# A two-layer, two-block network on one core: expert rows through a DRAM table and four indirect gathers, and a reordered start

## The chip, the cores and the metric

One NeuronCore of a Trainium2 chip runs one program, one launch. The metric is the device time of that program in microseconds (us), lower is better. TensorE (PE), VectorE (DVE), ScalarE (ACT), GpSimd (POOL) and SyncE (SP) run their own instruction streams and wait for each other by semaphores; transfers are issued by SP, ACT and POOL.

## The reference, cut to what matters

A first block (two layers of attention beside a long convolution) and a second block (two layers) are applied to 256 tokens of width 1024. All is float32. The change touches the very start of the first block (its RMS norm and its position bias) and the last stage of the second one, a mixture of experts:

```python
def moe_swiglu(h, w_router, w_gate, w_up, w_down):
    logits = (h @ w_router).astype(jnp.float32)
    top_val, top_idx = lax.top_k(logits, TOP_K)          # 2 of 8 experts for each token
    weights = jax.nn.softmax(top_val, axis=-1)
    gates = jnp.sum(jax.nn.one_hot(top_idx, N_EXPERTS, dtype=jnp.float32) * weights[..., None], axis=-2)
    out = jnp.zeros_like(h)
    for e in range(N_EXPERTS):
        out = out + gates[..., e:e + 1] * swiglu(h, w_gate[e], w_up[e], w_down[e])   # 1024 -> 2816 -> 1024
    return out
...
        y = moe_swiglu(h, o_router[j], o_exp_gate[j], o_exp_up[j], o_exp_down[j])
        x = x + (g * y).astype(x.dtype)
    return rmsnorm(x, final_norm).astype(x.dtype)
```

In the first block, `h = rms_norm(x, pre_norm[l])` opens each layer, `rel_bias[bucket]` gives the position bias of the attention, and the filters of the long convolution are `sin` layers times `exp(-t * |deltas|)` (the decay rates).

## The kernel before, in words

Every engine's stream is written by hand in one order; nothing reorders it. The program goes through the first block's two layers (a list of steps, `STEPS`), the even layer of the second block with a feed-forward of 11 chunks, the state-space layer, the router, and then the experts. All transfers of weights are issued by SP, in one order, each behind a wait for the slot of its ring to be free; small ones are issued by ACT.

**The expert loop.** The router's result is cut on the device into work items: an item is one expert and up to 96 of its tokens (`SLOTS`). With these inputs there are 8 items. The loop (`nc.Fori`, over a count read from `itab`) runs one item a turn on PE, ACT, DVE and SP. On PE an item is:

- `lone()`, one small job, and then 8 waves (`wave(w)`, 32 matmuls of 512 columns each in four column groups; a float32 matmul has two records in the trace, so 64 records): the up and gate products of the item's tokens with the expert's weights. The weights come in 11 chunks `wgu` of 2 MB in four slots.
- `lone_sum()` behind wave 0: it needs `xpart`, which ACT copies out of PSUM (`xp_ready`).
- **`back(i)`** behind wave 0: four 128x512 matmuls that add the rows of the *previous* item back to their tokens. Their left side is `ptb`, the one-hot matrix of who sits in which slot, turned by `turn_slots`; their result is scaled by the gate and added to `x` by DVE in `taken_back`. For item 0 the rows are zeros. One more `back` stands behind the loop.
- `turn(w)`, transposes of a wave's result; **`turn_slots(i)`** behind wave 1, four transposes of the one-hot matrix.
- `down(c)` for 11 chunks `wdn` of 1 MB, behind the waves.
- **`gather(i + 1)`** behind wave 7: 16 small matmuls that pick the next item's tokens; in the last item they pick nothing that is used.

SP issues a chunk when PE has let go of its slot: chunk 4 (`load_up(i, e, 4)`) waits for the end of wave 0, and wave 2 waits for that chunk. In the chunk numbers that wait first, wave 5 needs chunks 7 and 8 and wave 6 chunk 9.

DVE ends an item by writing `ysb`, the item's 96 rows scaled by the layer's gate (two operations of 128x512; the PSUM tile holds the 96 rows in six pieces of 32 partitions).

**The start.** SP issues x (1 MB), constants, weights chunk 0, more constants, weights chunks 1 to 3. ACT issues `rel_bias`, a table, `vec` (the norm gains and other vectors), `flt_deltas` (the decay rates, 1 MB) and `flt_w_out`; then copies and stores the bias row, then waits for x **and `vec`**, and squares x for the norm. Behind the norm it issues eight reads of the stored row (`skewed`), which PE needs at the step `bias` behind its third group of projections.

## Time and profile before

| | before |
|---|---|
| median of 3 runs | 2069.11 us (2068.7 to 2070.05) |
| the profiled execution, its own time | 2067.41 us |
| its span | 2065.6 us |
| mean granted TensorE clock | 0.985 of full speed |
| PE / DVE / ACT / POOL busy | 97% / 32% / 18% / 5% of the span |
| DMA, mean over the span | 229 GB/s |

Busy shares are means over stages with different limits. PE is the engine with nearly no idle time, so what matters for each part of a change is whether it stands in PE's stream, or makes PE wait.

### The profile page before, as it was taken

What the parts mean: (1) busy time and instruction counts of PE and PEld (TensorE: products, weight loads), DVE (VectorE), ACT (ScalarE), POOL (GpSimd) and SP (SyncE); (2) the same over time, 40 slices, a digit from 0 to 9 for tenths busy, and PEclk for the clock granted to TensorE, in tenths of its full rate; (3) what the DMA queues carried; (4) which work ended last, traced back from release to release, by engine and by line L of the source; (5) the groups of instructions that cost most, each with busy time, mean ns of one, the idle gap of its engine ahead of it and who ended that gap; (6) DMA issues with size and microseconds to landing.
All of it is one profiled execution on the core that took longest, in us unless ns stands there. A gap on an engine that the chain in (4) does not pass through costs nothing.

```text
span 2065.6 us, 28841 instructions
## 1 busy us (share of the span) xinstructions
PE 1998.3 (97%) x12128; PEld 1104.6 (53%) x12128; DVE 659.8 (32%) x1436; ACT 379.0 (18%) x784; POOL 111.1 (5%) x94
## 2 busy tenths in 40 slices
PE   6999999999998999999989988999999999999998
PEld 5577775667774865777756544232323333333332
DVE  3265113345212474344449934010101010111112
ACT  3212103212102232243320012010101010111101
POOL 0000000000000000000016610000000000000000
PEclk9999999999999999999999998999999999999999
DMA  8245575344665223243323125989898979797973
GB/s 316 82 163 204 217 282 202 116 156 171 234 265 228 82 82 150 115 175 131 123 102 123 41 102 217 376 329 374 324 384 330 381 309 403 311 402 298 406 299 148
DMA packets 41645, 472.71 MB, mean 229 GB/s; under 512 B 4676, under 2 KB 6340, under 8 KB 8040
## 3 DMA queue, kind: packets, MB, share of 16 engines
q1 hardware_dynamic: 39008, 465.44, 56.6%
q10 hardware_dynamic: 2568, 6.31, 0.9%
q8 instruction: 48, 0.79, 0.1%
q14 instruction: 21, 0.17, 0.0%
HBM read 470.68 MB, written 1.06 MB: 228 GB/s over the span
## 4 chain that ended last, share of the span: by engine, by line
PE 88%; DVE 7%; DMA 3%; issue 1%; ACT 0%; ACTq 0%; SPq 0%; POOLq 0%; POOL 0%; DVEq 0%
PE bank L898 21%; PE bank L551 14%; PE bank L928 11%; PE bank L850 7%; PE bank L862 3%; PE bank L714 3%; PE bank L543 3%; PE bank L536 3%; PE bank L720 3%; PE bank L564 2%; PE bank L978 2%; PE bank L970 2%; DMA arena<-in_wgu 1%; PE bank L617 1%; PE bank L649 1%; PE bank L1074 1%
## 5 line engine op out<-in xcount | busy, mean ns | idle before, releaser
L898 PE MATMUL bank<-arena 128*32 128x512 f32 x4096 | 453.1, 594 | 1.7 <-DMA arena<-in_wgu 1.7
L551 PE MATMUL bank<-arena 128*128 128x256 f32 x1408 | 312.6, 381 | 0.0
L898 PEld LDWEIGHTS bank<-arena 128*32 128x32 f32 x4096 | 130.3, 110 | 311.1 <-issue 296.3
L551 PEld LDWEIGHTS bank<-arena 128*128 128x128 f32 x1408 | 264.9, 190 | 53.7 <-issue 19.4
L928 PE MATMUL bank<-arena 128*32 128x512 f32 x2112 | 238.2, 595 | 0.0
L1993 DVE TENSOR_TENSOR arena<-arena,bank 128x256 f32<-128x256 f32 x64 | 27.0, 421 | 595.3 <-ACT arena L1406 540.4
L850 PE MATMUL bank<-arena 128*128 128x256 f32 x704 | 153.7, 379 | 0.1
L850 PEld LDWEIGHTS bank<-arena 128*128 128x128 f32 x704 | 133.6, 190 | 21.7 <-issue 4.1
L928 PEld LDWEIGHTS bank<-arena 128*32 128x32 f32 x2112 | 63.0, 110 | 133.2 <-issue 132.5
L1406 ACT ACTIVATE arena<-bank 128x256 f32<-128x256 f32 x64 | 24.5, 383 | 587.9 <-PE bank L898 587.9
L2207 POOL TENSOR_TENSOR arena<-arena 128x512 f32<-128x512 f32 x64 | 81.2, 1268 | 293.0 <-DVE arena L2040 290.5
L862 PE MATMUL bank<-arena 128*128 128x512 f32 x176 | 77.2, 592 | 0.0
L536 PE MATMUL bank<-arena 128*128 128x512 f32 x128 | 56.4, 596 | 1.8 <-ACT arena L1238 1.8
L714 PE MATMUL bank<-arena 128*128 128x256 f32 x256 | 56.8, 381 | 0.0
L720 PE MATMUL bank<-arena 128*128 128x512 f32 x128 | 56.4, 596 | 0.2 <-DVE arena L1886 0.2
L543 PE MATMUL bank<-arena 128*128 128x256 f32 x256 | 56.3, 381 | 0.0
L862 PEld LDWEIGHTS bank<-arena 128*128 128x128 f32 x176 | 33.5, 190 | 37.8 <-issue 37.3
L543 PEld LDWEIGHTS bank<-arena 128*128 128x128 f32 x256 | 48.3, 190 | 9.7 <-issue 3.4
L714 PEld LDWEIGHTS bank<-arena 128*128 128x128 f32 x256 | 48.3, 190 | 7.6 <-issue 0.8
L2195 POOL TENSOR_TENSOR arena<-arena 128x512 f32<-128x512 f32 x22 | 28.1, 1278 | 366.1 <-ACT arena L1238 366.1
L1057 PE MATMUL bank<-arena 32*128 32x256 f32 x128 | 37.4, 422 | 9.7 <-DVE arena L2040 9.0
L1972 DVE TENSOR_TENSOR arena<-arena,bank 128x256 f32<-128x256 f32 x22 | 9.3, 421 | 117.1 <-ACT arena L1381 117.1
(416 smaller groups left out, 1952.6 us busy)
## 6 DMA issues: line engine op xcount, KB each, us to landing
arena<-in_wgu SPq DMA_DIRECT2D x88, 2048.0 KB, 9.4
arena<-in_w SPq DMA_DIRECT2D x46, 2048.0 KB, 8.1
arena<-in_wdn SPq DMA_DIRECT2D x88, 1024.0 KB, 7.9
arena<-in_modw SPq DMA_DIRECT2D x24, 2048.0 KB, 10.2
arena<-in_wf SPq DMA_DIRECT2D x11, 3072.0 KB, 10.3
arena<-in_flt_deltas ACTq DMA_DIRECT2D x2, 1024.0 KB, 15.6
cst<-in_consts SPq DMA_DIRECT2D x1, 1162.0 KB, 17.3
arena<-in_x SPq DMA_DIRECT2D x1, 1024.0 KB, 5.3
```

What stands on the lines that cost most here:

```text
L536: ins = mm(bank[b][:, :], mT[:, k, h * P:(h + 1) * P], w[:, k * 512:(k + 1) * 512], start=(k == 0), stop=(k == KT - 1))
L543: ins = mm(bank[b][:, j * S:(j + 1) * S], w[:, col:col + P], y_in[:, k, :], start=(k == 0), stop=(k == 3))
L551: ins = mm(bank[b][:, j * S:(j + 1) * S], w[:, col:col + P], hT[:, k, :], start=(k == 0), stop=(k == KT - 1))
L564: ins = mm(bank[n % 2][r, :], band[:, k, 31 - c:63 - c], ring[at % RING][:, k * 512:(k + 1) * 512], start=(k < 4), stop=(k >= 4), skip_gro ...
L714: ins = mm(bank[n % 2][:, j * S:(j + 1) * S], w[:, col:col + P], hT[:, k, :], start=(k == 0), stop=(k == KT - 1))
L720: ins = mm(bank[n % 2][:, :], lhs(k), w[:, k * 512:(k + 1) * 512], start=(k == 0), stop=(k == KT - 1))
L850: ins = mm(bank[4 + f][:, u * S:(u + 1) * S], w[:, col:col + P], hT[:, k, :], start=(k == 0), stop=(k == KT - 1))
L862: ins = mm(bank[2 * t + i][:, :], hid[:, d % 2, f, t * P:t * P + P], w[:, col:col + 512], start=(d == 0 and f == 0), stop=(d == FFC - 1 an ...
L898: ins = mm(bank[w % 2][32 * j:32 * j + 32, :], hTe[:, k, TOK * b:TOK * b + TOK], wslot[c % RING][:, k, :], start=(k == 0), stop=(k == KT - ...
L928: return mm(bank[4 + n][32 * g:32 * g + 32, :], lhs, dslot[c % RING][:, f, n * 512:(n + 1) * 512], start=first, stop=last, skip_group_chec ...
L970: mm(bank[6 - 2 * t + n][:, :], ptb[:, n, t * P:(t + 1) * P], ysb[:, n, :], start=True, stop=True).then_inc(sm["back_ps"], 1)
L2207: ins = pool.tensor_tensor(cz[o % 4][:, n], zz[:, o % 2], tab[o][:, n, :].unsqueeze(1).broadcast_to([P, 2, S]), ALU.mult)
```

## The change

**Expert rows.** A table `slots` in DRAM has 96 rows of 1024 for each item. A loop item no longer adds the item before it: `back`, `turn_slots` and `taken_back` are gone from it. Instead DVE puts the 96 rows of the item together (two more operations of 32 partitions for each half), and ACT stores them with three transfers. The loop now runs over all items but the last, and the last item is written out behind it (`expert(last, True)`); it keeps `turn_slots` and one `back` for its own rows, has no `gather`, and in its waves DVE works out the table rows of each token (`token_rows`, 29 small operations), POOL gathers them with four indirect transfers of 128 rows, and DVE adds them (`rows_added`). Every row of the table is first given finite values by one transfer in DRAM of 6.29 MB (from the weights `w3[0:3]`), issued by SP in the feed-forward stage. The gates are no longer worked out before the loop.

**The start.** x comes in two transfers, `vec` is ACT's first one and is waited for only where the norm's result leaves PSUM; the square root's table is loaded while x is under way; the bias row is stored and the decay rates are asked for behind the squares; ACT's `Abs` of the decay rates stands behind the third sine, the `Silu` of the conditioning vector at the first value group. SP waits for the first constants before it asks for the others, and for weights chunk 0 before chunk 1. Some semaphores are merged.

```diff
@@ sync
-            sp.dma_start(x, a["x"].rearrange("b (t p) d -> p (b t) d", p=P)).then_inc(sm["x_landed"], 16)
+            tokens = a["x"].rearrange("b (t p) d -> p (b t) d", p=P)
+            for t, landing in enumerate(("x_landed", "x1_landed")):
+                sp.dma_start(x[:, t, :], tokens[:, t, :]).then_inc(sm[landing], 16)
             sp.dma_start(cst[:, 0:C_FC], a["consts"][:, 0:C_FC]).then_inc(sm["cst_landed"], 16)
             sp.dma_start(ring[0], a["w12"][0]).then_inc(landed[0], 16)
+            sp.wait_ge(sm["cst_landed"], 16)
             for at, end in ((C_FC, C_HOT), (C_LT, C_N)):
                 sp.dma_start(cst[:, at:end], a["consts"][:, at:end]).then_inc(sm["rest_landed"], 16)
+            sp.wait_ge(landed[0], 16)
             sp.dma_start(ring[1], a["w12"][1]).then_inc(landed[1], 16)
...
                     for i in range(2):
                         sp.dma_start(bst[i], a["b5"][:, i]).then_inc(sm["b5_landed"], 16)
+
+                    sp.dma_start(a["slots"].rearrange("i s d -> (i s d)").rearrange("(a b) -> a b", a=4 * P), a["w3"][0:3].rearrange("n p k -> (n p k)").rearrange("(a b) -> a b", a=4 * P))\
+                        .then_inc(sm["rows_out"], 16)
@@ tensor: expert
                     if w == 0:
                         lone_sum()
-                        back(i)
                     else:
                         if w == 1:
-                            pe.wait_ge(sm["acc_out"], i + 2)
+                            pe.wait_ge(sm["ysb_ready"], i * 2 + 2)
                         turn(w - 1)
-                    if w == 1:
-                        turn_slots(i)
+                    if w == 1 and final:
+                        turn_slots()
...
                 turn(WAVES - 1)
-                gather(i + 1)
+                if not final:
+                    gather(i + 1)
...
-            with nc.Fori(0, items_of(pe), engines=[pe.engine], hint_back_edge=True) as i:
+            last = last_of(pe)
+            with nc.Fori(0, last, engines=[pe.engine], hint_back_edge=True) as i:
                 expert(i)
-            back(items_of(pe))
+            expert(last, True)
+            back(last)
@@ scalar
                 squares(n)
+                if n == 0:
+                    bias_row()
+                    filter_loads(0)
+                if ready:
+                    act.wait_ge(sm["vec_landed"], ready)
...
                 turned(WAVES - 1)
+                if not final:
+
+                    act.wait_ge(sm["ysb_ready"], i * 2 + 4)
+                    for rows, cols, src in ((slice(0, SLOTS), slice(0, 512), ysb[0:SLOTS, 0, :]),
+                                            (slice(0, 2 * TOK), slice(512, D), ysb[2 * TOK:P, 1, :]),
+                                            (slice(2 * TOK, SLOTS), slice(512, D), ysb[0:TOK, 1, :])):
+                        act.dma_start(a["slots"][i][rows, cols], src).then_inc(sm["rows_out"], 16)
@@ vector: expert
                 for w in range(WAVES):
-                    if w == 3:
+                    if w == 3 and not final:
                         slots(i + 1)
+                    if w == 2 and final:
+                        token_rows(i)
+                    if w == WAVES - 2 and final:
+                        rows_added()
...
-                        taken_back(i)
-                link(v.tensor_copy(small[:, 46:48], pg.rearrange("p a b -> p (a b)")[:, bass.ds(i * 4 + 2, 2)]))
-                gathered(i + 1)
+                if not final:
+                    gathered(i + 1)
                 dve.wait_ge(sm["xdn_ps"], i * FFC + FFC)
+                dve.wait_ge(sm["rows_out"], i * (16 * 3) + 32)
                 for n in range(2):
-                    v.tensor_tensor(ysb[:, n, :], bank[4 + n][:, :], gateb[:, n * 512:(n + 1) * 512], ALU.mult)\
-                        .then_inc(sm["ysb_ready"], 1)
+                    gate = gateb[:, n * 512:(n + 1) * 512]
+                    ins = v.tensor_tensor(ysb[:, n, :], bank[4 + n][:, :], gate, ALU.mult)
+                    if not final:
+
+                        to, part = ((slice(2 * TOK, SLOTS), slice(SLOTS, P)), (slice(0, TOK), slice(TOK, 2 * TOK)))[n]
+                        link(ins)
+                        link(v.tensor_tensor(late[to, :], bank[4 + n][part, :], gate[part, :], ALU.mult))
+                        ins = v.tensor_tensor(ysb[to, n, :], ysb[to, n, :], late[to, :], ALU.add)
+                    ins.then_inc(sm["ysb_ready"], 1)
...
+            def rows_added():
+
+                dve.wait_ge(sm["rows_in"], 16 * 4)
+                for t in range(TT):
+                    for n, gate in enumerate((30, 36)):
+                        link(v.scalar_tensor_tensor(x[:, t, :], taken[:, n, t, :], small[:, gate + t:gate + t + 1], x[:, t, :],
+                                                    ALU.mult, ALU.add))
@@ gpsimd, behind its last work
+            pool.wait_ge(sm["row_of"], 1)
+            table = a["slots"].rearrange("i s d -> (i s) d")
+            for n in range(2):
+                for t in range(TT):
+                    at = ITEMS + 2 + 2 * n + t
+                    pool.indirect_dma_start(out=taken[:, n, t, :], out_offset=None, in_=table,
+                                            in_offset=bass.IndirectOffsetOnAxis(ap=itab[:, at:at + 1], axis=0))\
+                        .then_inc(sm["rows_in"], 16)
```

**PE, the first half of a loop item.** Of before, from wave 0 (`landed1`) to the transposes behind wave 1:

```order
L898 MATMUL bank<-arena 32x512 [waits landed1]
L898 MATMUL bank<-arena 32x512 x31
L887 MATMUL bank<-arena,cst 32x512 [waits xp_ready]
L969 ISA [waits pt_ready,hte_ready]
L970 MATMUL bank<-arena 128x512 [waits ysb_ready]
L969 REGISTER_ALU
L970 MATMUL bank<-arena 128x512 [waits ysb_ready]
L970 MATMUL bank<-arena 128x512 x2
L898 MATMUL bank<-arena 32x512 [waits landed2]
L898 MATMUL bank<-arena 32x512 x31
```

Of the change, the same place:

```order
L912 MATMUL bank<-arena 32x512 [waits landed1]
L912 MATMUL bank<-arena 32x512 x31
L901 MATMUL bank<-arena,cst 32x512 [waits xp_ready]
L912 MATMUL bank<-arena 32x512 [waits landed2]
L912 MATMUL bank<-arena 32x512 x31
L962 ISA
L918 ISA [waits ysb_ready]
L924 MATMUL bank<-cst,arena 128x128 [waits xlhid_ready,xhid_ready]
L924 MATMUL bank<-cst,arena 128x128
L926 MATMUL bank<-cst,arena 128x128 x2
```

The four matmuls of `back` (L970) are gone, and wave 1 stands right behind `lone_sum` (L887, now L901); behind wave 1 the `turn_slots` transposes no longer follow the four of `turn(0)`.

**ACT, the end of a loop item and, past the branch, what the next one begins with** (L1401, now L1429, copies `xpart`). Of before:

```order
L1397 ACTIVATE arena<-bank 128x256 [waits xtr_ps] x2
L1467 REGISTER_ALU
L1467 COMPARE_AND_BRANCH
```

Of the change, and then the head of the loop body, to which the branch goes:

```order
L1425 ACTIVATE arena<-bank 128x256 [waits xtr_ps] x2
L1447 ISA
L1451 ISA [waits ysb_ready]
L1451 DMA slot_rows<-arena 96x512
L1451 ISA
L1451 DMA slot_rows<-arena 64x512
L1451 ISA
L1451 DMA slot_rows<-arena 32x512
L1503 REGISTER_ALU
L1503 COMPARE_AND_BRANCH
```

```order
L176 ISA
L1428 REGISTER_ALU
L1429 ACT_TABLE_LOAD
L1429 ACTIVATE arena<-bank 128x512 [waits xp_ps]
L1431 ISA
L1434 ACT_TABLE_LOAD
```

A wait for `ysb` and three transfers now stand between an item's last copy and the next item's table load and copy of `xpart`.

**ACT, the start.** Of the change, from its first work on (the transfers of `vec`, `rel_bias` and the table stand ahead of it):

```order
L1131 ACTIVATE small<-small 1x1 [waits x_ready]
L1133 ACTIVATE arena,small<-arena 128x1024 [waits x_landed]
L1134 ACTIVATE small<-small 128x1 [waits act_chain]
L1139 ACTIVATE arena,small<-arena 128x512 [waits x1_landed]
L1140 ACTIVATE small<-small 128x1 [waits act_chain]
L1143 ACTIVATE arena,small<-arena 128x512 [waits act_chain]
L1144 ACTIVATE small<-small 128x1 [waits act_chain]
L1185 ACTIVATE arena<-bank 4x512 [waits row_ps]
L1186 DMA bias_rows<-arena 4x512 [waits act_chain]
L1174 DMA arena<-in_flt_deltas 128x2048
L1176 DMA arena<-in_flt_w_out 64x2048
L1159 ACTIVATE arena<-bank,vec 128x256 [waits xt_ps,vec_landed]
```

The squares of x now stand ahead of the copy and store of the bias row and ahead of the two large transfers, and the wait for `vec` has moved from the first square to the first copy of the norm's result.

## Rows read from the trace of the kernel before

**Rows 1.** The page: the DMA engines' busy share in tenths, in 40 slices.
```profile
DMA  8245575344665223243323125989898979797973
```

**Rows 2.** Stretches: length, busy PE, PEld, DVE, ACT, POOL; clock, DMA share, GB/s.
```profile
1571.66:1669.68 98.02, 98.02 (x858) 32.20 (x857) 11.89 (x28) 10.11 (x22) 0.00 (x0) 1.00 0.87 353
...
1566.00:1568.00 2.00, 2.00 (x24) 0.57 (x20) 0.00 (x0) 0.00 (x0) 0.00 (x0) 1.00 1.02 426
...
1578.00:1579.00 1.00, 1.00 (x13) 0.26 (x8) 0.00 (x0) 0.00 (x0) 0.00 (x0) 1.00 0.00 0
...
825.00:850.00 25.00, 24.96 (x116) 21.99 (x117) 2.51 (x6) 5.01 (x10) 0.43 (x2) 1.00 0.32 131
```

**Rows 3.** PE in order of time, one loop item: start us, us, what.
```profile
1571.59 3.70 PE L970 MATMUL bank<-arena 128*128 128x512 f32 x8
1575.22 7.07 PE L898 MATMUL bank<-arena 128*32 128x512 f32 x64
...
1582.72 0.60 PE L987 MATMUL bank<-cst,arena 128*128 128x128 f32 x4
...
1648.69 3.71 PE L978 MATMUL bank<-arena 128*128 128x96 f32 x32
...
1668.66 1.02 PE L887 MATMUL bank<-arena,cst 128*32 128x512 f32 x2
```

**Rows 4.** Chunk 4, issued by SP at 1571.0 and at 1669.1: us to landing.
```profile
DMA to landing us min/median/max: 7.8/7.8/7.8
...
DMA to landing us min/median/max: 8.1/8.1/8.1
```

**Rows 5.** DVE and ACT in order of time, around the end of an item.
```profile
1660.35 1.29 DVE L2003 TENSOR_TENSOR arena<-bank,arena 128x512 f32<-128x512 f32 x2 [4.56 <-PE bank L928]
...
1662.05 0.60 ACT L1401 ACTIVATE arena<-bank 128x512 f32<-128x512 f32 x1 [11.38 <-PE bank L880]
1662.66 1.28 ACT L1406 ACT_TABLE_LOAD   x1
```

**Rows 6.** The start in order of time.
```profile
12.51 1.06 ACT L1118 ACTIVATE arena<-arena 128x1024 f32<-128x1024 f32 x1 [3.07 <-DMA vec<-in_vec]
...
19.85 7.07 PE L551 MATMUL bank<-arena 128*128 128x256 f32 x32
20.79 3.72 ACTq L1167 DMA_DIRECT2D arena<-bias_rows  x8
...
29.14 1.90 ACT L1180 ACTIVATE arena<-arena 128x2048 f32<-128x2048 f32 x1
...
45.51 0.42 ACT L1245 ACTIVATE arena<-arena 64x256 f32<-64x256 f32 x1 [2.48 <-DVE arena L1579]
45.67 3.80 PE L580 MATMUL bank<-arena,cst 128*128 128x512 f32 x8 [1.68 <-DMA arena<-bias_rows]
```

**Rows 7.** Transfers: x, feed-forward chunks (page); weights chunk 0 (one issue).
```profile
arena<-in_x SPq DMA_DIRECT2D x1, 1024.0 KB, 5.3
...
arena<-in_wf SPq DMA_DIRECT2D x11, 3072.0 KB, 10.3
...
L372 SPq DMA_DIRECT2D arena<-in_w x1: 424/424/424, 1.7 to 1.7; - x1
...
DMA to landing us min/median/max: 11.0/11.0/11.0
```

**Rows 8.** The tail in order of time.
```profile
2056.97 1.98 PE L970 MATMUL bank<-arena 128*128 128x512 f32 x4 [1.49 <-issue]
...
2059.84 1.28 DVE L2179 SCALAR_TENSOR_TENSOR arena<-arena,small 128x1024 f32<-128x1024 f32 x1
```

**Rows 9.** SP in the feed-forward stage, and the chain of waits there.
```profile
822.12 1.17 SPq L404 DMA_DIRECT2D arena<-in_b  x2
859.80 145.09 SPq L399 DMA_DIRECT2D arena<-in_wf  x8
...
880.45 9.71 PE bank L850 x45
```

More of the change, by code:

```diff
@@ L313, in model @@
         pg = view(W + 9088, ITEMS, 4)
+        rowv = rk[:, 1, 0, 0:2, :]
+        rowm = rk[:, 1, 1, 0:2, :]
+        late = view(W + 3904, 512)
+        taken = view(W + 10752, 2, TT, D)
         uT = view(CH * 2, 8, S)
@@ L452, in _ @@
             sp.wait_ge(sm["items_ready"], 1)
[L453 removed]
+            last = last_of(sp)
             with sp.Fori(0, last) as i:
@@ L980, in gather, with turn_slots @@
                 ins.then_inc(sm["ga_ps"], 1)
-            def turn_slots(i):
-                pe.wait_ge(sm["hte_ready"], i + 1)
+            def turn_slots():
                 for n in range(2):
@@ L1116, in squares @@
                     act.wait_ge(sm["x_ready"], 1)
+                    F(small[0:1, 93:94], small[0:1, 95:96], ACT.Sqrt)
                     act.wait_ge(sm["x_landed"], 16)
@@ L1177, in _ @@
                         F(small[:, 2:4], bank[7][:, 0:2], ACT.Exp).then_inc(sm["lam_exp"], 1)
-                        act.wait_ge(sm["delta_landed"], l * 16 + 16)
-                        deltas = absd.rearrange("p a b -> p (a b)")
-                        F(deltas, deltas, ACT.Abs).then_inc(sm["absd_ready"], 1)
                     elif name == "norm":
-                        act.wait_ge(sm["vec_landed"], l * 16 + 16)
-                        norm(l, (2, 3, 4, 5), vec[:, V_PRE:V_PRE + 8], None)
+                        norm(l, (2, 3, 4, 5), vec[:, V_PRE:V_PRE + 8], None, l * 16 + 16)
                         if l == 0:
@@ L1245, in _ @@
                         F(fa[0:64, c, :], fa[0:64, c, :], ACT.Sin).then_inc(sm["f_sine"], 1)
+                        if c == 2:
+                            act.wait_ge(sm["filter_landed"], l * 32 + 32)
+                            deltas = absd.rearrange("p a b -> p (a b)")
+                            link(F(deltas, deltas, ACT.Abs))
                     elif name == "f_out":
@@ L1464, in _ @@
                   bias=mods[:, 72 + k:73 + k]).then_inc(sm["hta_ready"], 1)
-            act.dma_start(finb, a["final"].partition_broadcast(P)).then_inc(sm["fin_landed"], 16)
+            act.dma_start(finb, a["final"].partition_broadcast(P)).then_inc(sm["rows_out"], 16)
             act.wait_ge(sm["items_ready"], 1)
-            with nc.Fori(0, items_of(act), engines=[act.engine], hint_back_edge=True) as i:
+            last = last_of(act)
+            with nc.Fori(0, last, engines=[act.engine], hint_back_edge=True) as i:
                 link.restart()
                 expert(i)
+            link.restart()
+            expert(last, True)
             F(small[0:1, 93:94], small[0:1, 95:96], ACT.Sqrt)
@@ L1493, in norm @@
                     v.tensor_scalar(xn[:, 1, cols], x[:, 1, cols], small[:, 11:12], None, ALU.mult).then_inc(sm["xn_ready"], 1)
+                if ready:
+                    dve.wait_ge(sm["vec_landed"], ready)
                 for k in (0, 1, 4, 5):
@@ L2091, in taken_back, with token_rows @@
                                                      ALU.mult, ALU.add)
-                        if last and t + n:
+                        if t + n:
                             ins.then_inc(sm["x_part"], 1)
-                        elif t + n < 2:
-                            link(ins)
-                if not last:
-                    ins.then_inc(sm["acc_out"], 1)
-                    dve.wait_ge(sm["acc_out"], i + 2)
+            def token_rows(i):
+                link(v.tensor_tensor(gsel, selm, rsel, ALU.mult))
+                link(v.tensor_reduce(small[:, 44:46], gsel, AX.X, ALU.add))
+                link(v.reciprocal(small[:, 44:46], small[:, 44:46]))
+                link(v.tensor_tensor(gsel, gsel, small[:, 44:46].unsqueeze(2).broadcast_to([P, TT, 8]), ALU.mult))
+                link(v.tensor_tensor(cnt[:, 0, :], cnt[:, 2, :], cnt[:, 1, :], ALU.subtract))
+                link(v.tensor_scalar(cnt[:, 0, :], cnt[:, 0, :], float(SLOTS), 1.0, ALU.mult, ALU.add))
+                link(v.tensor_tensor(rowv, lg, cnt[:, 0, :].unsqueeze(1).broadcast_to([P, TT, 8]), ALU.add))
+                link(v.tensor_tensor(rowv, rowv, selm, ALU.mult))
+                one, two, g1, g2, keep, row2 = (small[:, c:c + 2] for c in (26, 24, 30, 28, 32, 34))
+                link(v.tensor_reduce(two, rowv, AX.X, ALU.max))
+                link(v.tensor_reduce(one, rowv, AX.X, ALU.add))
+                link(v.tensor_tensor(one, one, two, ALU.subtract))
+                for row, gate in ((two, g2), (one, g1)):
+                    link(v.tensor_tensor(rowm, rowv, row.unsqueeze(2).broadcast_to([P, TT, 8]), ALU.is_equal))
+                    link(v.tensor_tensor(rowm, rowm, gsel, ALU.mult))
+                    link(v.tensor_reduce(gate, rowm, AX.X, ALU.add))
+                link(v.tensor_scalar(small[:, 38:39], cnt[:, 3, 0:1], float(SLOTS), 0.5, ALU.mult, ALU.add))
+                link(v.tensor_scalar(keep, two, small[:, 38:39], None, ALU.is_lt))
+                link(v.tensor_tensor(small[:, 36:38], g2, keep, ALU.mult))
+                link(v.tensor_tensor(small[:, 46:48], g2, small[:, 36:38], ALU.subtract))
+                link(v.tensor_tensor(row2, two, one, ALU.subtract))
+                link(v.tensor_tensor(row2, row2, keep, ALU.mult))
+                link(v.tensor_tensor(row2, row2, one, ALU.add))
+                dve.wait_ge(sm["rows_out"], i * (16 * 3) + 32)
+                for n, row in enumerate((one, row2)):
+                    link(v.tensor_scalar(row, row, 1.0, None, ALU.subtract))
+                    ins = v.tensor_copy(itab[:, ITEMS + 2 + 2 * n:ITEMS + 4 + 2 * n], row)
+                    if n == 0:
+                        link(ins)
+                ins.then_inc(sm["row_of"], 1)
```

111 lines of the change are left out of this document (52 added, 59 removed).

## The prediction

> **What bounds the kernel now.** I read the page first: PE is busy in 97% of the span, so the question for every part is whether it stands in PE's stream. The one other resource that could bind is the DMA engines, busy in 9 of 10 tenths in most slices of the last third [rows 1], so I read that third by stretches. One loop item lasts 98.02 us, PE is busy in all of it, and the transfers move 353 GB/s at a share of 0.87; in a full stretch they move 426 GB/s, and just behind the start of an item there is a hole in which they move nothing [rows 2]. So the loop is bound by PE, with some 13% of DMA time to spare. Then I read PE in order of time in one item [rows 3], and for each wave the chunk that it waits for, with its issue and landing [rows 4]. Last I read the start, where PE is not yet bound by itself: its first projection starts at 19.85, and at 45.67 it has waited 1.68 us for the bias rows [rows 6].
>
> **The change part by part.** Durations are those of the profiled execution (2067.41 us of its own time); the median of the runs is 1.70 us above it, and I take the same sum off both.
>
> *`back` out of the loop.* Its matmuls start at 1571.59 and wave 1 at 1575.22, so it costs 3.63 us, with nothing of PE's beside it [rows 3]. Before there are nine of them (eight items and one behind the loop), after there is one: 8 x 3.63 = 29.0 us.
>
> *`turn_slots` out of seven items.* Its group is busy for 0.60 us, and successive groups overlap by 0.07 (3.70 busy for 3.63 of stream), so it takes 0.53 [rows 3]: 7 x 0.53 = 3.7 us.
>
> *`gather` out of the last item.* 3.71 less the same 0.07: 3.6 us [rows 3]. `down` behind it has its data, since in the last item SP has only three chunks to bring.
>
> *Does the weights stream allow it?* The first to be late would be chunk 4: it is issued at the end of wave 0, lands 7.8 or 8.1 us later [rows 4], and wave 2 needs it. From its issue at 1571.03 to wave 2 before are 12.2 us (1583.25 is where the group behind `turn_slots` begins: 1582.72 + 0.53). The change takes 4.16 us out of just this stretch, so 8.06 are left for 7.8 to 8.1. It fits, or costs up to 0.1 us an item. The later chunks are issued and needed on the same side of the removed work, so their distances stay. The three stores of an item add 0.39 MB, 0.9 us at 426 GB/s, and fall ahead of the hole [rows 2]. I take 0, and 1 us over the seven items as the other end.
>
> *What the loop gets in exchange.* DVE's two operations of `ysb` start at 1660.35 and take 1.29 together [rows 5]; now there are six. Each now waits for the one before it, so I price it at half of the 1.29 and 0.08 for the wait, 0.73, and `ysb` is whole at 1664.7. ACT waits for that, ahead of the next item's work. Its three issues cost 3.72 / 8 = 0.47 each [rows 6], which gives 1666.1, with register work and the branch about 1666.5. Then come the table load, 1.28, and the copy of `xpart`, 0.60 [rows 5]: 1668.4. `lone_sum` wants it at 1668.66 [rows 3]. Before, this copy was done at 1662.65, so 5.8 of its 6.0 us of cover are used up. PE's weight load for `lone_sum` goes ahead of the matmul, and the address work of the three stores has no row. The bounds are 0 and, with twice the issue time, 1.4 us an item; I take 0.3, being nearest to the computed edge: 7 x 0.3 = 2.1 us lost. DVE and ACT are otherwise idle for 88 and 90% of an item [rows 2], and the writes into `ysb` that wait for the last stores wait for something 90 us old.
>
> A rule of the Trainium skill speaks here. The row puts the table load at 1.28 us and the ACTIVATE ahead of it ends within 0.02 us of it (1662.05 + 0.60, then 1662.66) [rows 5]. The skill's page "ScalarE: Activation LUTs", section "What ACT_TABLE_LOAD costs", says that a switch costs a drain of 1380 ns on top of the 1283 ns of the load. By that rule `xpart` would be ready at 1669.8 and each of the seven borders would cost about 1.4 us more, 9.7 in all, a sum of 29.5 in place of 39.2. The row's 0.02 us gap speaks for the load alone.
>
> *The last item and the tail.* `token_rows` is 29 operations on at most 16 columns. At 0.60 us each, what ACT needs for 512 columns [rows 5], they would take 17 us; I estimate 0.2 each, 6 us. PE needs DVE's next product only two waves on, so both ends cost 0. The four gathers have no row in the trace. Below, they land as x did, 5.3 us each [rows 7], above, as the bias reads did, 21.6 us for eight (24.06 to 45.63, of which the landing at 45.63 is what the 1.68 us wait ends on) [rows 6]. They have from about 23 us into the item until wave 7's end near 80, less 5.3 us for `rows_added` (four at 1.28 [rows 8]): 52 us of cover, so 0 at either end. If that cover were gone, each us would cost one. The stall of 1.49 us that PE has behind the loop's end [rows 8] moves ahead of the last item: 0.
>
> *The fill of the table.* 6.29 MB read and as much written, issued by SP behind its two small loads, about 823.3 [rows 9]. Next in SP's queue is feed-forward chunk 3, issued at 859.80 and needed at 880.45 [rows 9]; it takes 10.3 us to land [rows 7]. So the fill may last until 870.1, 46.8 us. At 426 GB/s for both directions it needs 29.5 us, and the engines have a share of 0.68 free there [rows 2], 43 us. Nothing in the trace is a copy inside DRAM: at 426 one way it takes 14.8, and at half the two-way rate 59, which would cost 12. I take 0.
> The skill's page "DMA: Bandwidth & Descriptors", section "Latency and other measured facts", gives 207 GB/s down to 103 for copies between tensors in HBM, by the pitch of the rows. By that the fill takes 30 to 61 us, so 0 to 14 us lost. No run here shows a pitch of this kind.
>
> *The start.* Before, the first square starts at 12.51, held by `vec` [rows 6], while x has landed at 0.7 + 5.3 = 6.0 [rows 7]. After, half of x lands near 5, and the squares with the table already loaded end near 8.7. PE has its row product first, until 9.3, then the transposes until 11.4; ACT copies the row, issues three transfers (1.9 us) and evacuates from 12.0 on. Weights chunk 0 landed at 1.7 + 11.0 = 12.7 [rows 7] with more traffic beside it than now. So the first projection starts near 12.5 in place of 19.85: 7.3 us earlier, and PE comes to the bias step at 36.7 in place of 44.0. There it needs the bias rows. Their reads are now issued at 14 to 17 in place of 20.8, but the same bytes come ahead of them, and the decay rates, 1 MB, now stand later in the same queue. I put their landing at 38 to 41. The decay rates' `Abs`, 1.90 [rows 6], now stands on ACT between the third sine (45.51 before, 38.2 after) and the evacuations that the bias step waits for, and holds it until 44.1 in place of 49.47. So 5.4 is the most; the least is 0, if the bias rows land no earlier than now. I take 5.0.
>
> *Sum.* 29.0 + 3.7 + 3.6 + 5.0 - 2.1 = 39.2, and the profiled execution goes from 2067.4 to 2028.2, the median from 2069.1 to 2029.9.
>
> **The rivals.**
> *ACT holds the next item* (0.15). The stores and the table load end later than 1668.7. For it: 5.8 of 6.0 us of cover are used. Against it: PE needs only the one copy so early. At 1.4 us a border 7.7 us come back: 2037.6, and up to 2045 at 2.5.
> *The start gives nothing* (0.10). The bias rows land near 45 again, since the DMA engines are full until then. 5.0 come back: 2034.9.
> *The DMA engines bind the loop* (0.05). If 353 GB/s were what they can hold, 35.0 MB would take 99.1 us an item: then only the last item (3.6 + 3.6) and the start remain, less 7 x 1.1, and it ends at 2064.6. Against it: 426 GB/s in a full stretch, and the hole [rows 2].
> *The fill is late* (0.06). At 59 us it holds chunk 3 by 12 us: 2042.
> *Slower: the gathers* (0.03). `rows_added` blocks DVE, and with it PE behind wave 7. From 52 us after the row numbers are ready each us costs one; past 91 us for four gathers (23 us each) the change loses. Nothing in the rows comes near this for 2 MB beside a half-loaded queue; at 120 us it would be 2098.
>
> **How the numbers follow.** The forecast has 0.60, and with its own bounds (start 0 to 5.4, ACT 0 to 0.7 a border, chunk 4 up to 1) reaches from 2027 to 2037. The start's rival lies in that; the range goes down to 2024, should the evacuations at the start wait for less than I think, and up to 2041, which takes in the nearer half of ACT's rival. The far half, the fill, the DMA bound and the gathers are left out, under 0.2. All cases but the last are faster by over 0.2% (4 us), which is about what a measurement of this kernel can tell from no change: 0.96 faster, 0.01 within, 0.03 slower.
>
> **What would show it.** Loop items of 94 us, with wave 1 about 0.8 us behind wave 0 and no idle PE ahead of `lone_sum`; a wait there for ACT shows the rival. Wave 2 waiting for `in_wgu` shows chunk 4 late. PE's bias step begins near 39 to 40. Feed-forward chunk 3 without a wait on `in_wf`. In the last item no DVE wait for the gathers. The prediction is wrong if loop items stay above 96, or if a wait of over 5 us stands in the last item.

## The result, and the profile after

The changed kernel takes 2058.09 us (median of 7 runs, 2054.24 to 2064.75), the kernel before, run beside it, 2070.05 (7 runs, 2068.7 to 2075.71). The ratio is 0.9938, 95% interval 0.9922 to 0.9953. So the change gives 12 us, and not the 39.2 that were forecast; 2058.09 lies outside the range of 2024 to 2041. The profiled execution took 2056.35 us, with a span of 2054.5 and a mean granted clock of 0.980.

The slices of the page read as before [rows 1]: PE 96% busy, and in the last third the DMA engines at 8 to 9 tenths.

```profile
PE 1970.8 (96%) x12004; PEld 1088.6 (53%) x12004; DVE 657.8 (32%) x1432; ACT 372.7 (18%) x776; POOL 115.3 (6%) x98
...
DMA  8245565335466222734321225989898989898984
```

What is new stands in PE's list of waits (us in total, times, longest):

```profile
PE bank L912 <- DMA arena<-in_wgu: 19.0, 10, 2.7
PE bank L503 <- DVE arena L1526: 14.8, 5, 5.2
...
PE bank L595 <- DMA arena<-bias_rows: 6.0, 1, 6.0
...
PE bank L901 <- ACT arena L1429: 1.2, 6, 0.3
```

The waves (L912, before L898) wait 19.0 us for up chunks, ten times, where they waited 1.7 in all before. Eight of the ten waits stand at wave 5, one in each item (1.80 to 2.71 us); the other two stand at wave 2, which needs chunk 4, and come to 1.1 us together. The bias step waits 6.0 us where it waited 1.68 [rows 6]. The wait for ACT at the border of two items, which I had feared most, is 1.2 us.

PE in order of time in a loop item, as in [rows 3]. The item begins at `lone` (L894):

```profile
1460.45 1.90 PE L894 MATMUL bank<-arena 128*32 128x512 f32 x16
...
1477.86 7.07 PE L912 MATMUL bank<-arena 128*32 128x512 f32 x64
...
1500.36 7.05 PE L912 MATMUL bank<-arena 128*32 128x512 f32 x64
1507.34 0.44 PE L926 MATMUL bank<-cst,arena 128*128 128x128 f32 x2
1507.70 2.78 PE L942 MATMUL bank<-arena 128*32 128x512 f32 x24
1513.00 8.77 PE L912 MATMUL bank<-arena 128*32 128x512 f32 x64 [2.52 <-DMA arena<-in_wgu]
...
1558.92 1.47 PE L894 MATMUL bank<-arena 128*32 128x512 f32 x12
```

Wave 5 starts at 1513.00 after a wait of 2.52 us, and then takes 8.77 us in place of 7.05. The stretches of the same item say why (columns as in [rows 2]):

```profile
1460.50:1558.90 98.40, 95.67 (x848) 30.72 (x844) 11.55 (x26) 9.51 (x21) 0.00 (x0) 0.98 0.90 355
1509.00:1513.00 4.00, 1.49 (x16) 0.26 (x8) 0.00 (x0) 0.00 (x0) 0.00 (x0) 1.00 0.65 219
1513.00:1517.00 4.00, 4.00 (x24) 1.16 (x28) 0.00 (x0) 0.00 (x0) 0.00 (x0) 0.57 1.04 418
1517.00:1521.00 4.00, 4.00 (x44) 1.17 (x36) 0.00 (x0) 0.00 (x0) 0.00 (x0) 1.00 0.99 412
...
1512.00:1513.00 1.00, 0.00 (x0) 0.00 (x0) 0.00 (x0) 0.00 (x0) 0.00 (x0) 1.00 0.35 147
```

Behind the wait the granted clock is 0.57 of full speed for 4 us, then full again: most of that stretch ran at 1.2 GHz of 2.4. So the wait costs 2.52 + 1.72 = 4.24 us, and 98.40 - 4.24 = 94.2 is the item that was forecast. In the last microsecond of the wait the DMA engines are busy at a share of only 0.35, though SP has issued three more chunks by then (1510.7 to 1512.0): PE doesn't wait for bandwidth.

Not every wait has this second cost. Wave 5 of two later items, behind equal waits of 2.28 us:

```profile
1611.19 8.77 PE L912 MATMUL bank<-arena 128*32 128x512 f32 x64 [2.28 <-DMA arena<-in_wgu]
...
1709.37 7.07 PE L912 MATMUL bank<-arena 128*32 128x512 f32 x64 [2.28 <-DMA arena<-in_wgu]
```

Four of the eight waves behind such a wait take 8.71 to 8.77 us, the other four 7.07.

The chunk that wave 5 waits for is chunk 8. SP's issue of it and its landing, first in the kernel before (wave 5 there starts at 1517.65), then in the changed one:

```profile
L424 SPq DMA_DIRECT2D arena<-in_wgu x1: 332/332/332, 1508.6 to 1508.6; - x1
...
DMA to landing us min/median/max: 9.0/9.0/9.0
```

```profile
L439 SPq DMA_DIRECT2D arena<-in_wgu x1: 332/332/332, 1501.3 to 1501.3; - x1
...
DMA to landing us min/median/max: 11.6/11.6/11.6
```

Before, 9.0 us of landing stood against 9.05 us from issue to need: it fitted with nothing to spare. After, the distance is nearly the same (1513.00 - 2.52 - 1501.35 = 9.1) and the landing is 2.6 us longer.

The start, in order of time, with its stretches:

```profile
5.00 1.06 ACT L1133 ACTIVATE arena<-arena 128x1024 f32<-128x1024 f32 x1 [1.29 <-DMA arena<-in_x]
...
12.12 7.17 PE L566 MATMUL bank<-arena 128*128 128x256 f32 x32
...
14.78 3.73 ACTq L1194 DMA_DIRECT2D arena<-bias_rows  x8
...
45.92 5.41 PE L595 MATMUL bank<-arena,cst 128*128 128x512 f32 x8 [6.00 <-DMA arena<-bias_rows]
```

The first projection starts at 12.12 in place of 19.85, as forecast (12.5). The reads of the bias rows are issued 6 us earlier, and the last still lands at 45.9. PE leaves the step later than before, at 51.3 in place of 49.5: it takes 5.41 us in place of 3.80 [rows 6].

### The profile page after: what moved, and what is told of

It is laid out like the page before. It is cut to its first block, busy times and chain, and to the rows that moved or that the text cites. A ratio compares the mean times of both kernels' runs of the same rounds, so it can differ in the third digit from the quotient of the medians.

```text
span 2054.5 us, 28569 instructions
## 1 busy us (share of the span) xinstructions
PE 1970.8 (96%) x12004; PEld 1088.6 (53%) x12004; DVE 657.8 (32%) x1432; ACT 372.7 (18%) x776; POOL 115.3 (6%) x98
## 4 chain that ended last, share of the span: by engine, by line
PE 83%; DMA 8%; DVE 6%; issue 1%; ACTq 1%; ACT 1%; SPq 0%; POOL 0%; DVEq 0%
PE bank L912 17%; PE bank L566 14%; PE bank L942 10%; PE bank L865 7%; DMA arena<-in_wgu 5%; PE bank L877 4%; PE bank L729 3%; PE bank L558 3%; PE bank L551 3%; PE bank L735 3%; PE bank L579 2%; PE bank L991 2%; PE bank L632 1%; DMA arena<-bias_rows 1%; PE bank L664 1%; PE bank L1086 1%
## 5 line engine op out<-in xcount | busy, mean ns | idle before, releaser
L912 PE MATMUL bank<-arena 128*32 128x512 f32 x4096 | 464.9, 600 | 19.9 <-DMA arena<-in_wgu 19.0
L912 PEld LDWEIGHTS bank<-arena 128*32 128x32 f32 x4096 | 133.8, 111 | 332.4 <-issue 304.9
L942 PE MATMUL bank<-arena 128*32 128x512 f32 x2112 | 238.2, 595 | 0.0
## 6 DMA issues: line engine op xcount, KB each, us to landing
arena<-in_wf SPq DMA_DIRECT2D x11, 3072.0 KB, 10.4
arena<-in_flt_deltas ACTq DMA_DIRECT2D x2, 1024.0 KB, 11.6
```

The costliest lines, as they stand in the source:

```text
L912: ins = mm(bank[w % 2][32 * j:32 * j + 32, :], hTe[:, k, TOK * b:TOK * b + TOK], wslot[c % RING][:, k, :], start=(k == 0), stop=(k == KT - ...
L942: return mm(bank[4 + n][32 * g:32 * g + 32, :], lhs, dslot[c % RING][:, f, n * 512:(n + 1) * 512], start=first, stop=last, skip_group_chec ...
```

## The experiments

Ratios are against the kernel before, run on the same chip in the same job. "Item" is the time from one `lone` to the next in the profiled execution.

**e1: SP's order of transfers.**

```diff
-  ... (load_up, 7), (load_down, 5), (load_down, 6), (load_up, 8), (load_down, 7), (load_up, 9), (load_up, 10)
+  ... (load_up, 7), (load_up, 8), (load_down, 5), (load_down, 6), (load_up, 9), (load_up, 10), (load_down, 7)
```

> The changed kernel with one difference: in SP's list of an item's transfers, up chunk 8 stands ahead of the down chunks 5 and 6, and up chunks 9 and 10 ahead of down chunk 7. Each still waits for its own slot. Theory 1 (issue distance): in the changed kernel wave 5 waits about 2.3 us for chunk 8, because SP can't issue it before down(2), about 9 us ahead of the need, and the wait then makes the wave run at a lower granted clock for another 1.6 us. Then chunk 8 is issued some 6 us earlier here, the waits of 19.0 us on in_wgu go under 5, loop items come to 94 to 95 us, and the time is 2032 to 2038. Theory 2 (the DMA engines bind): the item's 35 MB can't come faster than in about 97 us, the order changes nothing but which wave waits, items stay at 97 to 98, and the time is 2054 to 2060.

Measured: 2033.31 us, ratio 0.9819 (0.9803 to 0.9835). The waits on up chunks fall to 0.8 us, and the item is 94.00 us with PE busy in 93.80 of it:

```profile
1507.01 7.05 PE L912 MATMUL bank<-arena 128*32 128x512 f32 x64
```

```profile
1457.20:1551.20 94.00, 93.80 (x848) 30.49 (x844) 11.54 (x26) 9.51 (x21) 0.00 (x0) 1.00 0.93 373
```

The first row is wave 5, with no wait and at full clock. The transfers move 373 GB/s where they moved 355: theory 1 holds, and theory 2, that the DMA engines bind, falls. Chunk 8 still takes 10.4 us to land here, but it is issued at 1491.8, 15 us ahead of its need.

**e2: lighter down chunks.** `dslot[...][:, 0:64]`, a 32nd of a chunk, for all down chunks but numbers 0 to 7 of the first item.

> The changed kernel with the down weights of all loop items after the first, and chunks 8 to 10 of each, brought as 64 of 2048 columns only (this leaves out the transfer of the rest, so the sums are taken over old weights); waits and order are untouched. The bytes of an item fall from 35 to 24 MB. Both theories of e1 expect the waits on in_wgu to vanish: items at 93.5 to 94.5, time 2030 to 2036. A third theory, that something else on the chip (the three stores of ACT, the table load) lengthens the item, expects items still over 96 and over 2048 us.

Measured: 2034.67 us, ratio 0.982 (0.980 to 0.984), later items 94.0 to 94.5. With a third of the bytes gone it is no faster than e1: the new order alone takes out all that the transfers cost. Theory 3 falls.

**e3: the same order in the kernel before.**

> The kernel before with the same new order of SP's transfers as e1. Theory 1: before, chunk 8 landed within about 0.1 us of when wave 5 wanted it, so PE hardly waited (1.7 us in all); the new order takes at most those 1.7 us: 2067 to 2070, the same within 0.2%. Theory 2 expects the same here. Slower than 2074 would say that the new order has a price of its own (the down chunks come late).

Measured: 2065.03 us, ratio 0.9972 (0.9962 to 0.9981): 5.9 us faster, more than expected. Its items take 97.8 in place of 98.0 to 98.7, and the first 100.8 in place of 102.0: the kernel before already paid for its late chunks. In the two profiles this is 3.3 us over the seven loop items (691.0 and 687.7); where the rest of the 5.9 comes from is not shown.

**e4: the old start.** The edits at the start undone in the changed kernel.

> The changed kernel with the start of the kernel before (x in one transfer, vec waited for ahead of the squares, conditioning and decay rates where they were; the merged semaphores stay). The prediction said that the new start is worth 5.0 us: then this takes 2063. The trace of the changed kernel says that its bias step begins 0.25 us later than before and runs at a lower granted clock, so that the new start costs 1.6 to 2 us: then this takes 2056 to 2057. In both cases the loop's share of the gain is what is left.

Measured: 2059.77 us, ratio 0.9951 (0.9933 to 0.9969), against 0.9938 (0.9922 to 0.9953) for the changed kernel. The forecast 5 us don't show, but the two intervals alone would not exclude them. **e8** asks the same on top of e1.

> The kernel of e1 with the start of the kernel before. The prediction priced the new start at 5.0 us: then 2038. If the bias rows land at the same time in both and PE's longer wait costs it clock, the new start loses 1 to 3 us: 2030 to 2032. If neither, 2033.

Measured: 2030.8 us, ratio 0.9809 (0.9779 to 0.9838), against 0.9819 (0.9803 to 0.9835) for e1: again no gain from the new start. The profiles settle it better than the times. PE leaves the bias step at 51.3, 53.1 and 53.4 us with the new start (changed, e15, e1) and at 49.5, 50.9 and 49.4 with the old one (before, e4, e8). And the first `lone` of the expert loop starts at 1264.4 to 1269.2, mean 1266.6, in eight profiles with the new start (changed, e1, e2, e6, e9, e14, e15, e17), and at 1262.3 to 1269.1, mean 1264.4, in eight with the old one (before, e3, e4, e5, e8, e10, e12, e13). A start worth 5 us would have it 5 us earlier. Those of e4 and e8 also show that a wait can cost clock or not: the bias step of e8, then that of e4, behind waits of nearly the same length.

```profile
45.59 3.80 PE L592 MATMUL bank<-arena,cst 128*128 128x512 f32 x8 [1.82 <-DMA arena<-bias_rows]
```

```profile
45.45 5.40 PE L592 MATMUL bank<-arena,cst 128*128 128x512 f32 x8 [1.94 <-DMA arena<-bias_rows]
```

The granted clock of the two steps is 1.00 and 0.69.

**e5: `back` alone out of the kernel before.**

```diff
                         lone_sum()
-                        back(i)
```

In DVE's stream `taken_back` goes with it: for all items but the last it only signals that it is done.

> The kernel before without the eight back of its items (the rows of all items but the last are not added to x: this work is left out); turn_slots, gathers and the old order of SP's transfers stay, there is no table, no store and no indirect gather. It asks why the removed 3.6 us came back in the changed kernel. Theory A: because PE alone ran into chunk 8, whose landing has no slack: then it happens here too, waits on in_wgu are over 8 us in all, items take 96 to 97.5, and the time is 2058 to 2066. Theory B: because what the change added (stores, table, indirect gathers) makes the chunks land 2.3 us later: then chunk 8 lands after 9 us as before, the waits stay under 4 us, items take 94.3 to 94.8, and the time is 2042 to 2048.

Measured: 2038.05 us, ratio 0.9845 (0.9812 to 0.9878), waits of 3.7 us on up chunks. So the 29.0 us for `back` came out (31.5), with the old order. Theory A falls: 3.6 us less of PE's work don't by themselves run into chunk 8. What theory B says of landings, waits and items holds, its time of 2042 to 2048 doesn't. The first down chunk behind the hole, issued 27.8 us into the item in both, first in e5, then in the changed kernel:

```profile
L433 SPq DMA_DIRECT2D arena<-in_wdn x1: 333/333/333, 1482.2 to 1482.2; - x1
...
DMA to landing us min/median/max: 4.9/4.9/4.9
```

```profile
L448 SPq DMA_DIRECT2D arena<-in_wdn x1: 333/333/333, 1488.2 to 1488.2; - x1
...
DMA to landing us min/median/max: 7.6/7.6/7.6
```

A transfer ends with 16 completions. Of this one in the changed kernel 13 come 4.4 to 4.7 us after the issue, one at 6.0 and two at 7.6; in e5 all have come by 4.95. The chunks behind it carry the lag on. Of chunk 8 in the same item 14 completions have come by 9.85 us and the last two come at 11.45 and 11.61: without these two PE would have waited an estimated 0.7 us in place of 2.52. What makes them late was the question of the next runs.

**e6: no stores. e9: no indirect gathers. e10: e5 with indirect gathers.**

> The changed kernel without the three stores of each loop item (so the table keeps what it was filled with: the rows of all items but the last are left out of the sum); the wait for ysb, the fill and the four gathers stay, and the old order of SP's transfers. Theory A (PE runs into chunk 8 by itself): as the changed kernel, waits on in_wgu of 15 to 20 us, 2054 to 2060. Theory B (the stores make the chunks land later): chunk 8 lands after 9 us, waits under 5 us, 2034 to 2042.

> The changed kernel (old order of SP's transfers) with the four indirect gathers of GpSimd replaced by four plain transfers of SP of the same size, from fixed rows of the table (so the rows added to a token aren't its own: the choice of rows is left out). Fill and stores stay. 
> The kernel of e5 (before without its eight back; the rows of all items but the last are left out) plus four indirect gathers of GpSimd of 128 rows each, issued behind the last item's last down, into a tile that is no longer used. Theory C expects that the mere presence of the gathers brings the late landings into the loop: items of 96 to 98.5, waits on in_wgu over 10 us, 2054 to 2062. Theory D expects items of 94.4 as in e5 and 2038 to 2042 (the gathers may add up to 3 us at the end).

Measured: e6 2054.83 us (ratio 0.9921, 0.9890 to 0.9951), e9 2060.36 (0.9953, 0.9939 to 0.9967), e10 2038.7 (0.9846, 0.9831 to 0.9862). The gathers are not the cause in either direction: theory C falls. The kernel of e10 has the lag once all the same, in its second item (96.9 us): the first down chunk behind the hole lands after 6.75 us, chunk 8 after 11.4. So the lag can come without anything that the change put into the loop, but rarely. Without the stores (e6, waits of 15.8 us) it stays, so they alone are not the cause, but in some items it is gone by chunk 8.

**e12: e5 with the table and its fill. e13: with the table and a small write. e14: `turn_slots` kept. e15: the changed kernel again. e17: e6 and e14 in one.**

> The kernel of e5 (before without its eight back; the rows of all items but the last are left out) plus the table in DRAM and its fill of 6.29 MB at the same place as in the changed kernel; no stores, no gathers. In e5 the first down chunk behind the hole landed 4.95 us after its issue at 27.8 us into the item, in the changed kernel 7.3 to 7.7 us after the same issue at the same time. Theory D1 (the table's place in DRAM or its fill is what makes the chunks late): that chunk lands after 7 us, waits on in_wgu over 10 us, 2054 to 2062. Theory E (it is something in the changed expert code itself): 4.9 us, waits under 5 us, 2036 to 2041.

> As e12, but of the table only the first item's 96 rows are written, once (0.39 MB in place of 6.29). If e12 shows the late landings, this tells the table's place in DRAM (late here too, 2054 to 2062) from the fill (not late, 2036 to 2041). If e12 doesn't, this is 2036 to 2041 too.

> The changed kernel with the four transposes of turn_slots back in every loop item (their result is used in the last one only). PE comes to wave 2 0.53 us later in each item, as in e5. Theory E1: the 0.53 us decide whether the engines stay in step: landings of 5 and 9 us, waits under 5 us, 2037 to 2043. Otherwise: landings of 7.5 and 11.5 us, waits of 12 to 20 us, 2054 to 2062.

> The changed kernel again, beside the three others on the same chip, as their yardstick: 2054 to 2062, with landings of 7 to 7.7 us for the first down chunk behind the hole in nearly all items.

> The changed kernel (old order of SP's transfers) without the three stores of an item (the rows of all items but the last are left out) and with turn_slots kept in every item: e6 and e14 in one. Each alone left the late landings in about half of the items (2054.8 and 2056.7). Theory F: both shift the moment at which the 16 engines run dry, and the late landings depend on such moments: then most items are free of waits here and it takes 2037 to 2046. Theory G: another part of the changed expert code is the cause: 2052 to 2058.

Measured: e12 2037.84 us (0.9848, 0.9832 to 0.9864), e13 2036.76 (0.985, 0.9831 to 0.9869), e14 2056.72 (0.9927, 0.9904 to 0.9951), e15 2058.48 (0.9944, 0.9923 to 0.9966), e17 2046.52 (0.9890, 0.9871 to 0.9908). The lengths of the seven loop items, from the starts of `lone` in the timelines:

```
before          102.0   98.7   98.1   98.0   98.0   98.1   98.1
changed          97.7   98.3   98.5   98.2   96.5   98.6   96.4
e15, the same    97.3   98.7   96.0   98.3   95.8   98.9   98.2
e9               99.9   95.9   99.0   98.7   96.4   98.9   98.4
e6              102.6   94.8   98.0   98.7   94.7   95.5   94.4
e14              97.3   97.3   95.2   94.6   94.8   99.0   99.3
e17              97.2   94.8   94.4   97.6   95.7   94.5   94.4
e5               97.0   94.5   94.4   94.5   94.4   94.3   94.4
e12              98.6   94.9   94.4   94.3   94.3   94.4   94.3
e1               95.5   94.2   94.0   94.0   94.0   94.0   94.0
```

Most items with the old order and without `back` are either near 94.5 or at 96 to 99. The table's place in DRAM and its fill are out (D1 falls). Items of 96 us or more are seven in the changed kernel, six in e15 and in e9, four in e14 (`turn_slots` kept), three in e6 (no stores), two in e17 (both), and the first alone in e5 and e12. Theory E1 falls by its time, and neither e14 nor e6 is told apart from the changed kernel by its interval. Only e17, with both parts, is, and the down chunk behind the hole still takes 5.3 to 7.5 us there, against 4.7 to 5.4 in e12. So both parts together move how often the lag comes, theories F and G each hold in part, and what starts it stays open. The new start is no cause: e4 has the old one, and waits of 18.3 us.

**e7, e11, e16, e18: the start, on top of e1.** SP asks for weights chunks 2 and 3 only behind the bias rows; e11 and e18 (one kernel) also have `Abs` behind the first sine; e16 has the old start with SP's wait.

```diff
+            sp.wait_ge(sm["biasr_landed"], 16 * 8)
             for r in range(2, RING):
                 sp.dma_start(ring[r], a["w12"][r]).then_inc(landed[r], 16)
...
-                        if c == 2:
+                        if c == 0:
                             act.wait_ge(sm["filter_landed"], l * 32 + 32)
```

> The kernel of e1 with one more wait on SP: weights chunks 2 and 3 (4 MB) are asked for only when the eight reads of bias rows have landed. Theory: at the start the DMA engines are full (over 400 GB/s from about 5 to 45 us) and the bias rows land last, at 45 to 49, in whatever order the rest is issued. With 6 MB fewer ahead of them they land near 31. PE then waits for no DMA at the bias step, but for ACT's work there, and begins it near 42 to 44: 3 to 6 us less, 2027 to 2031. Rival: the chunks 2 and 3 are then late, or the time from the norm to the bias step is bound by something else: 2032 to 2036.

> The kernel of e7 with ACT's Abs of the decay rates behind the first sine in place of the third, where ACT is idle for 9 us. In e7 PE waited 3.7 us for ACT at the bias step. Theory: Abs, 1.9 us, was what held it: the bias step begins 1.9 us earlier, PE loses less clock, 2025 to 2026.5. Rival: the wait at the bias step is for the evacuation behind the turned tokens alone, 2028 as e7.

> The kernel of e8 (new order in the loop, start of the kernel before) with SP's wait for the bias rows ahead of weights chunks 2 and 3, as in e7. Theory: what the new start can give is seen only once the bias rows are not the last to land. Here PE comes to the bias step near 42.5 and waits for nothing; e11 comes there at 37.9 and leaves it at 43.3. So this takes 2028.5 to 2031, 3 to 5 us more than e18. Rival: the two starts are equal here too (the wait for ACT takes the place of that for DMA): within 1 us of e18.

> The kernel of e11 again (new order in the loop, weights chunks 2 and 3 behind the bias rows, Abs behind the first sine), beside e16 as its yardstick: 2023 to 2027.

Measured: e7 2027.91 us (0.9801, 0.9770 to 0.9832), e11 2025.08 (0.9786, 0.9766 to 0.9805), e16 2029.29 (0.9805, 0.9790 to 0.9821), e18 2023.69 (0.9784, 0.9764 to 0.9804). In e11, in order of time:

```profile
31.64 0.81 SPq L391 DMA_DIRECT2D arena<-in_w  x2
...
37.90 1.88 PE L596 MATMUL bank<-arena,cst 128*128 128x512 f32 x4
...
41.49 1.98 PE L596 MATMUL bank<-arena,cst 128*128 128x512 f32 x4 [1.71 <-ACT arena L1211]
```

SP is through its wait at 31.64, so the bias rows had landed by then, 14 us earlier than in the changed kernel, and the step begins at 37.90 with no wait for a transfer. Against e16 in the same job the new start, with `Abs` moved, is now worth 5.6 us. Without that move it is not told apart from the old start by its time (e7, 0.9801, against e16, 0.9805), though in the profiles PE leaves the bias step at 45.8 in e7 and at 50.0 in e16. The rival of e16 falls. That of e7 is not excluded by the interval (2022 to 2035 us); against it stands that PE no longer waits for the bias rows and leaves their step 7.6 us earlier than in e1. That of e11 is not excluded by the times (2027.91 and 2025.08 overlap), but the wait for ACT falls from 3.67 to 1.71 us. e18 is the fastest kernel found: 2.2% less than before, and by the two ratios 1.5% less than the changed one.

## Why the prediction was wrong, step by step

- *`back` out of the loop, 29.0 us.* Right: 31.5 in e5 (25 to 39 by its interval), and the item of e5 is 94.30 us for 98.02 before [rows 2].
- *`turn_slots`, 3.7 us.* Item of e1 94.00, of e5 94.30, with 0.2 us an item of waiting for ACT added in e1: 0.5 an item, as priced.
- *`gather` out of the last item.* From the last `lone` to the end it is 111.3 us before and 103.9 in e1 (1927.2 to 2031.1): 7.4 for one `back` and one `gather`, 7.2 forecast.
- *ACT at the border, 2.1 us.* 1.2 us at six borders. The Trainium skill's rule of a drain on top of each table load ("ScalarE: Activation LUTs", "What ACT_TABLE_LOAD costs") would have made it 9.7 more; the trace shows no such time: behind the copy of `xpart` (1468.78 + 0.60) the next table load starts at 1469.40, takes 1.28, and ACT's next operation starts at 1470.69.
- *The fill.* Its 6.29 MB land 30.2 us after the issue at 825.4, inside the 46.8 us of cover, and feed-forward chunk 3 is not waited for. That is 208 GB/s read and as much written, near the 207 GB/s per direction that the Trainium skill's "DMA: Bandwidth & Descriptors", "Latency and other measured facts", gives for the smallest row pitch that it lists. The gathers cause no wait either.
- *"Does the weights stream allow it?"* **This step failed.** I priced chunk 4 alone, and that price held (1.1 us of waits in all, where I had 0 to 1). Of the rest I wrote that the later chunks "are issued and needed on the same side of the removed work, so their distances stay". The distances did stay. What I didn't read is that for chunk 8 the distance was used up: 9.05 us for a landing of 9.0, because SP held it behind two down chunks that PE needs only at 1532.0, 31 us later. And I took the landing for a constant, while here it grew by 2.6 us; in e5, where it didn't grow, nearly the same distance cost 3.7 us of waits in all. That cost 19.0 us of waits, where e1 has 0.8, and 6.9 us of lower clock behind them (the waves' busy time is 464.9 us against 458.0 in e1): 25.1, against the 24.8 us between the medians of the changed kernel and e1 and the 24.5 us between their seven loop items. My sign of being wrong, items above 96, came true.
- *"I put their landing at 38 to 41."* **The second step that failed.** The bias rows were issued 6 us earlier, but into DMA engines that are full from 10 to 40 us (share 1.00 to 1.04) and move the same 16 MB in the first 50 us as before. They landed at 45.9 (47.5 in e15, 47.2 in e1), not at 38 to 41, and the start gave nothing (e4, e8) in place of 5.0; by the profiles it lost some 2 us. This was my rival "the start gives nothing"; the clock lost behind the longer wait was in no rival.
- The 13% of DMA time "to spare" was a mean over an item. It says that the loop isn't bound by bandwidth, which held (373 GB/s in e1), and nothing of whether one chunk lands in time.

- *The sum.* 39.2 less 5.0 for the start and 25.1 for chunk 8 is 9.1, against a measured 12.0 (9.7 to 16.1 by the interval).

With both steps mended (e11, e18) the kernel is 44 to 46 us faster than before. That is no proof of the 39.2: 5.9 of it belong to the order itself (e3), and the wait on SP and the moved `Abs` are not part of the change either. In e1, with the order alone mended, it is 37.6; less 5.9 that leaves 31.7, where the prediction without its start has 34.2 and the start lost some 2.

## What to carry to other kernels

When work is taken out of the bounding engine's stream, read for every transfer of the loop two numbers, from issue to need and from issue to landing, and not only for those whose distance shrinks: one with 0.05 us to spare is late as soon as anything makes landings longer. Look at what the issuing queue holds a transfer behind; moving the urgent one ahead of those with time to spare was worth 25 us here and cost nothing. Reads issued 6 us earlier into full DMA engines landed no earlier here (45.9 for 45.6); with 4 MB of weights held back behind them they had landed by 31.6 (e11).

## What the runs showed of the hardware

- A wait of 2 to 3 us of PE can cost nearly as much again: behind a wait of 2.52 us the clock was granted at 0.57 for 4 us. Whether it falls isn't certain: of eight waits of 1.80 to 2.71 us in the changed kernel four were followed by a wave of 8.71 to 8.77 us in place of 7.05, four by one of 7.07, and two waits of 2.28 us went either way. At the start, waits of 1.82 and 1.94 us were followed by 1.00 and 0.69.
- The 16 parts of one transfer can complete up to 3 us apart, so that a 1 MB chunk lands after 7.6 us in place of 4.9 when it is issued at the same point of the item (changed kernel and e5). The lag passes on to the transfers behind it, chunk 8 included (11.6 us). Leaving out stores of 0.39 MB an item and adding 0.5 us of PE work together made it rarer (e17, 2046.5 us for 2058); what starts it was not found.
